# A third place for the raw weight halves of a decoder step, taken from the ring of sample chunks

## What is computed

```python
h = _rmsnorm(x, g_mix)
z = h @ w_in
u, va, q, k, v, gate_a, gate_b = jnp.split(z, cuts, axis=-1)
a = mix_a(gelu(u), rmsnorm(gelu(va)), w_s, b_s)
b, kv_states = mix_b(q, k, v)
merged = sigmoid(gate_a) * (a @ w_oa) + sigmoid(gate_b) * (b @ w_ob)
x = x + merged @ w_o
x = x + jnp.square(jax.nn.relu(rmsnorm(x) @ w_ff1)) @ w_ff2
x = x + sigmoid(rmsnorm(x) @ w_ple_gate) * (pe @ w_ple_proj)
```

## Time and profile before

| | us |
|---|---|
| median of 3 runs | 1088.68 |
| lowest and highest run | 1087.53, 1090.81 |
| the profiled execution, by its own time | 1087.71 |
| its span, first to last instruction | 1086.0 |
| PE busy | 1048.0 |
| DVE busy | 690.6 |
| ACT busy | 483.9 |
| POOL busy | 248.6 |

### The profile page before, as it was taken

The page is one execution under the profiler, slowest core; times in us unless marked ns, Lnnn a source line. Parts: engine busy times, 40 slices in busy tenths (PEclk is TensorE's granted clock), DMA queues, the critical chain, the costliest instruction groups (busy, mean ns, idle before and its releaser), DMA issues.

```text
span 1086.0 us, 21532 instructions
## 1 busy us (share of the span) xinstructions
PE 1048.0 (96%) x8507; PEld 1034.6 (95%) x8508; DVE 690.6 (64%) x881; ACT 483.9 (45%) x1181; POOL 248.6 (23%) x390
## 2 busy tenths in 40 slices
PE   8999999998989989989999999999999999999996
PEld 8999999998989989989999999999999999999996
DVE  5679888987878778989674354434443444345552
ACT  6773878568734564243264453213312421343331
POOL 2441323027310005857301210001000100112300
PEclk9999999999999999999999999999999999999999
DMA  6557655777687554675742245655554556465412
GB/s 198 198 171 234 204 186 167 255 222 208 235 234 242 169 197 130 200 235 155 262 144 78 79 135 194 200 167 183 191 193 163 183 196 198 164 199 165 161 48 83
DMA packets 130834, 196.20 MB, mean 181 GB/s; under 512 B 32208, under 2 KB 108272, under 8 KB 128960
## 3 DMA queue, kind: packets, MB, share of 16 engines
q1 hardware_dynamic: 105808, 122.46, 35.5%
q0 software_dynamic: 10816, 64.36, 18.5%
q10 hardware_dynamic: 14128, 8.26, 2.6%
HBM read 186.07 MB, written 62.00 MB: 228 GB/s over the span
## 4 chain that ended last, share of the span: by engine, by line
PE 67%; DVE 13%; ACT 5%; issue 5%; DMA 4%; SPq 4%; POOL 1%; ACTq 0%; DVEq 0%; POOLq 0%
PE gm L1101 52%; DMA w_raw<-in_w_in 3%; PE gm L1077 3%; PE gm L1078 3%; PE gm L1079 3%; DVE kv L1501 2%; DVE w_lo L1380 2%; SPq L533 2%; DVE kv L1542 1%; ACT prob L947 1%; ACT sq L657 1%; SPq L581 1%; DVE acc L1548 1%; POOL st L1917 1%; ACT w_hi L638 1%
## 5 line engine op out<-in xcount | busy, mean ns | idle before, releaser
L1101 PE MATMUL gm<-h_hi,w_hi 128*128 128x272 f32 x1088 | 228.3, 291 | 2.9 <-ACT z L688 2.6
L638 ACT CAST w_hi<-w_raw 128x1024 fp32r<-128x1024 f32 x150 | 150.6, 1044 | 171.6 <-PE gm L1101 116.5
L1101 PE MATMUL gm<-h_hi,w_lo 128*128 128x272 f32 x1088 | 225.6, 289 | 0.0
L1101 PE MATMUL gm<-h_lo,w_hi 128*128 128x272 f32 x1088 | 224.8, 288 | 0.0
L1380 DVE TENSOR_TENSOR w_lo<-w_raw,w_hi 128x1024 fp32r<-128x1024 f32 x150 | 178.3, 1227 | 45.8 <-ACT w_hi L638 43.8
L1077 PE MATMUL gm<-w_hi,h_hi 128*128 128x256 f32 x640 | 188.2, 294 | 5.1 <-issue 5.1
L1078 PE MATMUL gm<-w_hi,h_lo 128*128 128x256 f32 x640 | 182.2, 285 | 0.0
L1079 PE MATMUL gm<-w_lo,h_hi 128*128 128x256 f32 x640 | 181.4, 283 | 0.0
L1101 PEld LDWEIGHTS gm<-h_hi,w_hi 128*128 128x128 f32 x1088 | 170.8, 188 | 3.8 <-issue 3.3
L1101 PEld LDWEIGHTS gm<-h_lo,w_hi 128*128 128x128 f32 x1088 | 171.4, 189 | 0.0
L1101 PEld LDWEIGHTS gm<-h_hi,w_lo 128*128 128x128 f32 x1088 | 170.3, 189 | 0.0
(11 more groups left out here) (264 smaller groups left out, 1535.1 us busy)
## 6 DMA issues: line engine op xcount, KB each, us to landing
w_raw<-in_w_ff SPq DMA_DIRECT2D x64, 512.0 KB, 5.1
out_kvs<-in_cache_kv_w POOLq DMA_DIRECT2D x64, 510.0 KB, 4.3
w_raw<-in_w_in SPq DMA_DIRECT2D x60, 512.0 KB, 6.7
kv<-in_cache_kv_w SPq DMA_DIRECT2D x128, 128.0 KB
kv<-in_cache_kv_w SPq DMA_DIRECT2D x64, 256.0 KB
out_kvs<-in_cache_kv_w POOLq DMA_DIRECT2D x32, 508.0 KB, 4.8
kv<-in_cache_kv_w POOLq DMA_DIRECT2D x128, 64.0 KB, 3.3
w_raw<-in_w_o SPq DMA_DIRECT2D x8, 512.0 KB, 4.4
```

The lines of the kernel that those rows point to most:

```text
L638: nc.scalar.copy(w_hi[:, r, hh * 1024:(hh + 1) * 1024], w_raw[:, hh]).then_inc(w_hi_done, 1)
L1101: last = nc.tensor.matmul(gm[:, 2 * b2 + half, 0:HALF], w, x[:, k0 + k, half * HALF:(half + 1) * HALF], start=first, stop=end)
```

## The change

The ring of chunks goes from five to four places. The freed 4 KB per partition become `w_raw3`, a third place for raw halves. From panel 1 to panel 26 the halves, numbered 2p+hh, go to the places in turn (`raw_slot`); before and after, half hh goes to place hh. A half waits for the split of the half that had its place before (`raw_before`), now the third last. SP's order is changed with it: slot 3p loads the second half of panel p+1 and the first half of panel p+2. All the slots in which chunks are loaded follow from `RING` and come one chunk later; `CHUNKS_IN_SLOT` stays.

```diff
--- before.py
+++ after.py
@@ -129,6 +129,29 @@
     return j % 2 if paired(j) else 0
+P_THREE = 27
+def raw_slot(p, hh):
+    return (2 * p + hh) % 3 if 1 <= p < P_THREE else hh
+HALVES = [(p, hh) for p in range(P_FF + 1) for hh in range(2)]
+def raw_before(p, hh):
+    mine = [2 * x + y for x, y in HALVES if 2 * x + y < 2 * p + hh and raw_slot(x, y) == raw_slot(p, hh)]
+    return mine[-1] if mine else None
+def raw_count(p, hh):
+    return 16 * sum(1 for x, y in HALVES if 2 * x + y <= 2 * p + hh and raw_slot(x, y) == raw_slot(p, hh))
+THIRD_LAST = max(2 * p + hh for p, hh in HALVES if raw_slot(p, hh) == 2)
 NEXT_IN_BANK = {j: next((x for x in range(j + 1, len(PIECES)) if score_bank(x) == score_bank(j)), None) for j in range(len(PIECES))}
 MASKED_BY_ACT = [x for x in NEXT_IN_BANK.values() if x is not None]
@@ -139,7 +162,7 @@
     for _kind in ("keys", "values"):
         CHUNKS += [(_kind, _g, _j, 2) for _j in range(0, KEYS[_g], 2)] + [(_kind, _g, KEYS[_g], 1)]
 NCH = len(CHUNKS)
-RING = 5
+RING = 4
 CHUNKS_IN_SLOT = ("000000000101202202102102102102213122102102102102112111"
                   "112103121010030112010100120313200000000000")
 CHUNKS_AT = {_s: int(_n) for _s, _n in enumerate(CHUNKS_IN_SLOT)}
@@ -261,7 +284,7 @@
         A_F = A_O + 3 * OB
         A_X = A_O + KD * NT * 4
         A_R = A_F + 4096 + 8192
-        A_S = A_R + RING * 4096
+        A_S = A_R + RING * 4096 + 4096
         ends = [0]
         def sb(name, shape, dt, at):
@@ -271,7 +294,9 @@
         h_hi = sb("h_hi", [128, KD, NT], F32R, A_H)
         h_lo = sb("h_lo", [128, KD, NT], F32R, A_H + KD * NT * 4)
-        w_raw = sb("w_raw", [128, 2, 1024], F32, A_W)
+        w_raw2 = sb("w_raw", [128, 2, 1024], F32, A_W)
+        w_raw3 = sb("w_raw3", [128, 1024], F32, A_R + 16384)
+        raw = [w_raw2[:, 0], w_raw2[:, 1], w_raw3[:]]
         w_hi = sb("w_hi", [128, 2, 2048], F32R, A_W + 8192)
         w_lo = sb("w_lo", [128, 2, 2048], F32R, A_W + 8192 + 16384)
         z = sb("z", [128, 2, NT], F32, A_C)
@@ -363,7 +388,7 @@
             return ctx.enter_context(nc.semaphore(name))
-        w_landed = [sem("w_landed0"), sem("w_landed1")]
+        w_landed = [sem("w_landed0"), sem("w_landed1"), sem("w_landed2")]
         w_hi_done, w_lo_done = sem("w_hi_done"), sem("w_lo_done")
         unit_ready, unit_out, z_used = sem("unit_ready"), sem("unit_out"), sem("z_used")
@@ -428,6 +453,12 @@
             nk = 1024 // n
             return t[name].rearrange("(k p) n -> p k n", p=128)[:, hh * nk:(hh + 1) * nk, c0:c0 + n]
+        def raw_landed(pp, hh):
+            if isinstance(pp, int) and pp < P_FF:
+                return raw_count(pp, hh)
+            return (pp - P_FF) * 16 + raw_count(P_FF, hh)
         CONSTS, CONSTS2 = 16 * 9, 16 * 5
         def bc(ap, axis, n):
@@ -511,14 +542,22 @@
         @block.sync
         def _(sp):
-            def load_panel(p, j=None, pp=None):
-                pp = p if pp is None else pp
+            def load_half(p, hh):
+                freed = raw_before(p, hh)
+                if freed is not None:
+                    sp.wait_ge(w_lo_done, freed + 1)
+                if raw_slot(p, hh) == 2 and freed is None:
+                    sp.wait_ge(h_lo_done, KD + 1)
+                nk = 1024 // (COLS.get(PANELS[p][0], 256) if p < P_FF else 256)
+                x = raw_slot(p, hh)
+                sp.dma_start(raw[x].rearrange("p (k n) -> p k n", k=nk), wview(p, hh) if p < P_FF else wview(0, hh, 0)).then_inc(w_landed[x], 16)
+            def load_panel(p, j, pp):
                 for hh in range(2):
-                    if not (isinstance(pp, int) and pp == 0):
-                        sp.wait_ge(w_lo_done, 2 * (pp - 1) + hh + 1)
-                    nk = 1024 // (256 if j is not None or p >= P_PG else COLS.get(PANELS[p][0], 256))
-                    sp.dma_start(w_raw[:, hh].rearrange("p (k n) -> p k n", k=nk), wview(p, hh, j)).then_inc(w_landed[hh], 16)
+                    sp.wait_ge(w_lo_done, 2 * (pp - 1) + hh + 1)
+                    sp.dma_start(raw[hh].rearrange("p (k n) -> p k n", k=4), wview(p, hh, j)).then_inc(w_landed[hh], 16)
             def load_chunk(n):
@@ -543,7 +582,8 @@
             for a in range(2):
                 sp.dma_start(xn[:, a], t["x_prompt"][128 * a:128 * a + 128]).then_inc(x_tile_in[a], 16)
-            load_panel(0)
+            load_half(0, 0)
+            load_half(0, 1)
             for a in range(2, 4):
                 sp.dma_start(xn[:, a], t["x_prompt"][128 * a:128 * a + 128]).then_inc(x_tile_in[a], 16)
             sp.dma_start(xs[:], t["x_sample"]).then_inc(x_tile_in[4], 16)
@@ -553,8 +593,12 @@
                 sp.dma_start(dst[:], t[name].partition_broadcast(128)).then_inc(const_in, 16)
             for s in range(SLOTS):
                 p, kind, g, i, sub = UNITS[s]
+                if s == 0:
+                    load_half(1, 0)
                 if sub == 0 and p + 1 < len(PANELS):
-                    load_panel(p + 1)
+                    load_half(p + 1, 1)
+                    if p + 2 < len(PANELS):
+                        load_half(p + 2, 0)
                 if s == 0:
                     for i, name in ((1, "g_ffn"), (2, "g_ple")):
                         sp.dma_start(gcol[:, i], t[name].rearrange("(k p) -> p k", p=128),
@@ -595,6 +639,7 @@
                 if s == 86:
                     sp.wait_ge(values_used, kind_count(NCH - 1))
                     sp.dma_start(xn[:], t["x_prompt"].rearrange("(b p) d -> p b d", p=128)).then_inc(x2_in, 16)
+                    sp.wait_ge(w_lo_done, THIRD_LAST + 1)
                     sp.dma_start(xs[:], t["x_sample"]).then_inc(x2_in, 16)
                     sp.wait_ge(t_ready, TINDEX[("sb",)] + 1)
                     sp.dma_start(pn[:], t["p_prompt"].rearrange("(b p) d -> p b d", p=128)).then_inc(p_in, 16)
@@ -632,10 +677,11 @@
             def split_hi(pp, r, free):
                 for hh in range(2):
-                    act.wait_ge(w_landed[hh], (pp + 1) * 16)
+                    x = raw_slot(pp, hh) if isinstance(pp, int) and pp < P_FF else hh
+                    act.wait_ge(w_landed[x], raw_landed(pp, hh))
                     if hh == 0 and free is not None:
                         act.wait_ge(unit_ready, free)
-                    nc.scalar.copy(w_hi[:, r, hh * 1024:(hh + 1) * 1024], w_raw[:, hh]).then_inc(w_hi_done, 1)
+                    nc.scalar.copy(w_hi[:, r, hh * 1024:(hh + 1) * 1024], raw[x]).then_inc(w_hi_done, 1)
             def stage_slot(u):
@@ -1377,7 +1423,8 @@
                 for hh in range(2):
                     dve.wait_ge(w_hi_done, pp * 2 + (hh + 1))
                     cols = slice(hh * 1024, hh * 1024 + 1024)
-                    vec.tensor_tensor(w_lo[:, r, cols], w_raw[:, hh], w_hi[:, r, cols].bitcast(F32),
+                    x = raw_slot(pp, hh) if isinstance(pp, int) and pp < P_FF else hh
+                    vec.tensor_tensor(w_lo[:, r, cols], raw[x], w_hi[:, r, cols].bitcast(F32),
                                       ALU.subtract).then_inc(w_lo_done, 1)
             def shape_kq(u):

```

## The result

The change made the kernel slower: 1110.19 us median (1107.07 to 1111.76, 4 runs) against 1088.72 (1087.53 to 1090.81, 4 runs), a ratio of 1.0193 with a 95% interval of 1.0164 to 1.0221. The forecast was 1091.5, within 1084 to 1099. The profiled execution has a span of 1110.2 us, 24.2 more than before.

What follows compares the result with a forecast made beforehand. PE, busy 1048.0 of 1086.0 us, was taken as the bound. The terms 2.1+4.2-5.1+1.4 and 0.2 for late chunks gave +2.8 on the median 1088.68, so 1091.5 us, range 1084 to 1099.

Steps and rivals of the forecast that it cites:

- Term 1: Start: panel 1's first half waits for the last h_lo write, so PE starts panel 1 late; +2.1 us.
- Term 2: Slots 32 to 36: ring of four makes chunk 32 land late, stalling DVE, then ACT and PE; +4.2 us.
- slots 15 to 17: Chunks of these slots come late while DVE is full; +0.2 us.
- Term 3: Panels 18 to 21: halves issued earlier shorten ACT's cast waits and PE's stalls; -5.1 us.
- The rival that the third place does nothing: SP's order keeps each second half where it was, the panels 18 to 21 gain is 0; 1096.6 us, chance 0.17.
- Term 4: Last chunks: late chunk before panel 31's split costs +1.4 us; the second load of x_prompt costs zero.
- Slower: Sign of the outcome: a time above 1092.0 us, chance 0.47.
- the farthest rival: The ring is the bound: chunk 32 flies as long as panel 18's halves, DVE stands; 1099.2 us, chance 0.15.
- The rival of short flights: Loads land before they are wanted, as those at 14 us did; -1.8 us, 1086.9 us, chance 0.08.

Runs made afterwards that it cites:

- gains first: The changed kernel with the two gain-column loads issued ahead of the first half of panel 1; ratio 1.0117, 1099.9 us.
- x first: The changed kernel with the second loads of x_prompt and x_sample and those of p_prompt and p_sample ahead of panel 33's first half; ratio 1.0172.
- from panel 2: The changed kernel with the third place first used for panel 2's second half, panel 1 loaded as in the kernel before; ratio 1.0131.
- chunk 32 early: The kernel with the third place from panel 2, with chunk 32's load moved to slot 35, ahead of V loads and halves; ratio 1.0079.
- two places: The kernel before with only the ring cut to four: two raw places, old queue order; ratio 1.0094, 1097.6 us.
- two, chunk 32 early: Ring of four with two raw places and the load of chunk 32 in slot 35; ratio 1.0065 to the kernel before.

## Why the prediction was wrong

**Term 1, the start (2.1; it was 8.2).** The wait, the issue at 25.2 and the flight were right: the second half landed at 30.3, 31.1 was said, and with the gains in front PE is 1.7 late. The step that failed is the list of what is queued behind the waiting load: it named the second half, the first half of panel 2 and the chunks, "which are due later". The two gain loads stood there as well, in the diff's own lines, and they were due at once. They are tiny, and the columns they bring are wanted only in the feed-forward part, hundreds of us later; but POOL's wait counts them with the others. The run with the gains first gave 6.5 of the 8.2 us back. The place to look was POOL's wait, not the reader of the data.

**Term 2, the ring at chunk 32 (4.2; it was 5.5).** The mechanism, the place and the chain through DVE, ACT and PE came out as described. DVE stood 5.50 us and not 7.0, since after chunk 31 it was later than worked out, while the chunk landed 7.8 us after the start of its issue. PE was held 6.5 and lost 8.3 with the lower clock, and got 2.9 back at the next stalls. The sum let the clock's loss vanish and took one fall of 1.7 back besides; the stall of 3.3, said to be nearly gone, is still 1.96. The 0.2 for "slots 15 to 17" was 1.1: DVE waited for chunks 6 and 9 there, 1.3 us each. It isn't sure that the 1.1 comes of that: in the run with the gains first these waits were 1.07 and 0.81, and PE lost nothing up to unit 36.

**Term 3, panels 18 to 21 (-5.1; it was -0.6).** The sum counts from PE's lateness in front of panel 18, 14.73: 2.9 early behind panel 18, of which 2.45 are left behind panel 19, and 5.1 early behind panel 21. Panel 18 came as forecast: the stall went from 4.49 to 2.79 (2.7 was said) and the clock gave 1.0 (1.1), together -2.7. Panel 19 nearly did: the second half goes out 14.7 us behind the first one's old place, 331.14, behind four V loads that went out 14.9 later than before,

```profile
337.06 8.71 SPq L625 DMA_DIRECT2D V<-out_kvp  x4
345.81 2.41 SPq L554 DMA_DIRECT2D w_raw<-in_w_in  x2
...
353.59 1.04 ACT L684 CAST w_hi<-w_raw 128x1024 fp32r<-128x1024 f32 x1 [5.10 <-DMA w_raw<-in_w_in]
```

and it is cast 15.0 behind the old 338.57. So a half did take the place of the half before it, and PE is 2.2 early behind panel 19. The step that failed is panel 21, where the sum has the split "ready 4.3 early, less about 0.9" for late chunks, so PE "let go 3.4 early", and the clock staying up for "another 1.7". There too the second half took the first one's place: it goes out 13.2 behind the old 366.99 and is cast at 392.08, 13.3 behind the old 378.77, 1.0 later than the sum wants. But DVE was kept by two late chunks of the ring:

```profile
387.15 1.23 DVE L1589 TENSOR_TENSOR kv<-kv,sc 128x1024 f32<-128x1024 f32 x1 [1.04 <-DMA kv<-in_cache_kv_w]
...
391.02 1.23 DVE L1589 TENSOR_TENSOR kv<-kv,sc 128x1024 f32<-128x1024 f32 x1 [1.39 <-DMA kv<-in_cache_kv_w]
...
393.43 2.35 DVE L1427 TENSOR_TENSOR w_lo<-w_raw,w_hi 128x1024 fp32r<-128x1024 f32 x2
...
397.69 0.49 PE L1147 MATMUL gm<-h_hi,w_hi 128*128 128x272 f32 x2 [2.84 <-ACT z L734]
...
400.83 1.16 PE L1303 MATMUL psS<-kT,qT 64*128 64x128 f32 x8 [1.40 <-ACT psS L1000]
```

That is 2.4 us where 0.9 was booked. PE is let go 1.9 early and not 3.4; its stall is 2.84, as long as before (2.58) and not 1.6, and a second one of 1.40 follows, which was 0.32. And the clock falls as it did before: the granted clock is 0.92 from 392 to 413 us, 21 x 0.08 = 1.7 us. So PE comes out 1.6 later than it came.

How much of this is the third place's? Here are the profiled executions of the kernels with a ring of four, in us that PE gains from unit 53 on:

| up to | changed | gains first | x first | from panel 2 | chunk 32 early | two places | two, chunk 32 early |
|---|---|---|---|---|---|---|---|
| unit 55 (in panel 18) | 2.7 | 2.3 | 2.8 | 2.9 | 2.4 | 2.3 | 1.7 |
| unit 59 (in panel 19) | 2.2 | 2.2 | 2.3 | 2.9 | 3.6 | 1.0 | 0.3 |
| unit 64 (panel 22) | 0.6 | 2.5 | 2.5 | 0.4 | 2.7 | 3.2 | -0.5 |

At panel 18 at most 1.2 us is the third place's. At panel 19 it is 1 to 3 us ahead, and behind panel 21 nothing is left that goes beyond the scatter, and nowhere 5.1. A third place beside a ring of five was not tried, since there are no 4 KB per partition left for it; that it is neutral is shown for the ring of four only. The rival that the third place does nothing was nearest in its number for this term, but not by its mechanism, which kept each second half where it was.

**Term 4, the end (1.4 and zero; it was 2.7 and 5.1).** DVE waits 1.66 and 0.41 for late chunks and PE 1.50 in front of panel 31, of the size that was said; behind it comes a wait of 0.75 for DVE's `acc`, which was not in the sum.

```profile
537.37 1.23 DVE L1589 TENSOR_TENSOR kv<-kv,sc 128x1024 f32<-128x1024 f32 x1 [1.66 <-DMA kv<-in_cache_kv_w]
...
545.13 0.49 PE L1147 MATMUL gm<-h_hi,w_hi 128*128 128x272 f32 x2 [1.50 <-issue]
```

The failed step is the "zero" for the second load of x_prompt. It compared its issue with its reader at 545, leaving out that PE waits for x_sample too (landed at 542.2 before, where x_prompt landed at 538.1, so the slack was 3 us, not 7), and that the load would fly beside two halves. And 1.7 us were lost in panels 25 to 28 that no term had; the other six executions of the table above lose between -0.5 and 1.0 there, so it may be scatter, and its cause stays open.

**The rivals.** None of the rivals was the result: they varied the size of terms, and two of the losses (6 us at the start, 5 at the end) were in none. Slower had a chance of 0.47, but the farthest rival ended at 1099.2. The rival of short flights is refuted. It is what the fit of the Trainium skill gives ("DMA: Bandwidth & Descriptors", "Anatomy of one DMA — SWDGE (gpsimd) path"): it has a half land 3.2 us after its issue, an estimate. The page fits transfers of the GpSimd path, and these are SP's; the traces here have 3.3 to 16.7, so they come near it only for a transfer nearly alone.

## What to carry over

When a wait is put in front of a load in an in-order queue, list every instruction behind it up to the next one that already waited as long, and for each the semaphore that it counts up, not the data it brings: whoever waits for a sum of loads waits for the last. When two edits meet on one engine, cost the delay of the one where the gain of the other is to pass: here late chunks stand on DVE in front of the split that the earlier half should have freed. And book a clock that stays up only when the stall that is left has been worked out with both. A shorter ring hurts where its refill stands behind other loads; here moving one load by one slot gave back 5.7 us (3.2 with two places). And a block of tiny copies in front of big loads costs the queue as much per load as big ones: the eight of 0.2 KB took SP 0.77 us each, the six chunk loads of 256 KB behind them 0.64. Look for stretches with a DMA share near zero.

## What the runs showed of the hardware

The flight of a half of 512 KB varies at one and the same size with what flies beside it: 3.6 us in a quiet stretch (the first half of panel 34, before), 7.4 and 7.2 for those of panel 19, and 14.3 to 16.7 for the same two when they go out 9 to 11 us earlier into a full stretch. The two gain loads of 4 KB needed 6.0 and 6.1 us from issue to landing, where the three halves of 512 KB in front of them needed 3.6, 4.7 and 6.5.

After the gap of 6.60 us PE comes back at the lower level of its clock, 1.2 GHz (granted clock 0.50 from 37 to 40 us, 1.00 again from 44 on): 0.55 us for the first matmul, 0.41 for the next ones, where the gap of 1.41 left the clock at 1.00 and them at 0.28. It costs 1.5 us after the gap of 6.6, so the longest gap of a group is worth more than its own length.
